# Three edits to one kernel: gated delta net's k normed ahead of q, memory attention's result cut in its last rounds, one sum for two chained norms

## The reference, cut to what matters

```python
qh, kh, vh = l2norm(heads(qc)), l2norm(heads(kc)), heads(vc)     # gated delta net: q and k as unit rows
...
x = x + memory_cross_attention(rmsnorm(x, norm_xa_w), rmsnorm(mem, norm_mem_w), w_xq, w_xkv, w_xo)
#   4 heads of width 256: o = softmax(q k' / 16) v, then o @ w_xo
...
x = x + jnp.square(jax.nn.relu(h @ w_ff1)) @ w_ff2
x = rmsnorm(x, norm_out_w)                # the first block's last step
...
h = rmsnorm_2(x, g_mix); z = h @ w_in_2   # the second block's first
```

## Time and profile before

| what | value |
|---|---|
| runs of the kernel, us | 4253.4, 4267.21, 4269.94 (median 4267.21) |
| profiled execution, its own time | 4255.12 us |
| its span in the profile | 4253.6 us |
| TensorE busy | 3916.8 us (92% of the span) |
| VectorE / ScalarE / GpSimd busy | 2141.3 / 1153.0 / 329.8 us |
| mean granted TensorE clock | 0.943 of full speed |

### The profile page before, as it was taken

How to read it: one execution, slowest core, us unless ns; L and a number is a source line. 1 busy time by engine, 2 the same in 40 slices (tenths; PEclk the granted TensorE clock), 3 DMA queues, 4 the chain that set the end, 5 groups by cost and what they waited for, 6 DMA issues and landing times. The chain is left out here.

```text
span 4253.6 us, 75535 instructions
## 1 busy us (share of the span) xinstructions
PE 3916.8 (92%) x33542; PEld 3211.7 (76%) x33542; DVE 2141.3 (50%) x3526; ACT 1153.0 (27%) x1595; POOL 329.8 (8%) x362
## 2 busy tenths in 40 slices
PE   6999969988989999999999899778887999999999
PEld 5888847777858888888798677666666788888877
DVE  4643335554434444444624332555554476666673
ACT  4221234433323212212400322333323321111132
POOL 0001102330000000000000000231311000000000
PEclk8999979998999999999999899787888999999999
DMA  5211120114121111111232312211005211111111
GB/s 180 89 52 58 55 92 10 29 33 142 45 80 55 50 50 50 50 50 44 98 97 97 122 55 86 82 36 45 23 10 171 89 50 40 60 40 50 50 45 65
DMA packets 212888, 278.83 MB, mean 66 GB/s; under 512 B 15548, under 2 KB 170940, under 8 KB 212436
## 3 DMA queue, kind: packets, MB, share of 16 engines
q1 hardware_dynamic: 181040, 201.84, 14.9%
q10 hardware_dynamic: 31524, 72.16, 4.5%
HBM read 215.54 MB, written 58.43 MB: 64 GB/s over the span
## 5 line engine op out<-in xcount | busy, mean ns | idle before, releaser
L436 PE MATMUL ps<-sb_a_h,sb_whi 128*128 128x512 f32 x2784 | 1105.3, 397 | 6.0 <-DVE sb_wlo L397 5.5
L438 PE MATMUL ps<-sb_a_h,sb_whi 128*128 128x512 f32 x2784 | 1089.6, 391 | 0.0
L437 PE MATMUL ps<-sb_a_h,sb_wlo 128*128 128x512 f32 x2784 | 1089.2, 391 | 0.0
L436 PEld LDWEIGHTS ps<-sb_a_h,sb_whi 128*128 128x128 f32 x2784 | 525.6, 189 | 133.1 <-issue 15.8
L437 PEld LDWEIGHTS ps<-sb_a_h,sb_wlo 128*128 128x128 f32 x2784 | 525.7, 189 | 112.2 <-issue 4.5
L438 PEld LDWEIGHTS ps<-sb_a_h,sb_whi 128*128 128x128 f32 x2784 | 525.0, 189 | 112.5
L389 ACT ACTIVATE sb_whi<-sb_wraw 128x2048 fp32r<-128x2048 f32 (+3 forms) x146 | 260.3, 1783 | 825.1 <-PE ps L438 500.4
L397 DVE TENSOR_TENSOR sb_wlo<-sb_wraw,sb_whi 128x2048 fp32r<-128x2048 f32 (+3 forms) x146 | 313.9, 2150 | 238.9 <-ACT sb_whi L389 218.3
L548 DVE TENSOR_TENSOR sb_x<-sb_x,ps 128x512 f32<-128x512 f32 x480 | 313.5, 683 | 216.5 <-PE ps L438 207.6
L436 PE MATMUL ps<-sb_a_g,sb_whi 128*128 128x512 f32 x896 | 349.7, 390 | 10.5 <-DVE sb_x L548 10.5
L438 PE MATMUL ps<-sb_a_g,sb_whi 128*128 128x512 f32 x896 | 348.6, 389 | 0.0
(11 more groups left out here) (524 smaller groups left out, 5797.9 us busy)
## 6 DMA issues: line engine op xcount, KB each, us to landing
sb_wraw<-w_in SPq DMA_DIRECT2D x33, 1024.0 KB, 5.3
sb_wraw<-w_ff SPq DMA_DIRECT2D x32, 1024.0 KB, 5.3
sb_wraw<-w_up SPq DMA_DIRECT2D x22, 1024.0 KB, 5.1
sb_wraw<-w_down SPq DMA_DIRECT2D x11, 1024.0 KB, 5.0
...
```

Of the source, the lines that this page charges most:

```text
L436: e.matmul(o, wh[:, k, c], xh[:, sl], start=(k == 0), stop=False)
L437: e.matmul(o, wl[:, k, c], xh[:, sl], start=False, stop=False)
L438: m = e.matmul(o, wh[:, k, c], xl[:, sl], start=False, stop=(k == t.nk - 1))
```

## The change

1. Gated delta net. The gate rows are loaded by SyncE at the end of the stage before, ahead of the barrier, and to another place. SyncE loads k, then q, then v. The rows are squared, summed, rooted and multiplied in the order 3, 4, 5, 0, 1, 2: ScalarE does Ln of k's 6 halves, Exp of its 3 rows, then Ln of q's 6 halves and Exp of its 3 rows. The transposes of k wait for the third multiplied row instead of the sixth.
2. Memory attention. Once the last queries are done, SyncE loads the stored rows 0 to 5 back, each onto the place of its own low part. In round 8 rows 0 and 1 are cut, in round 9 rows 2 and 3, in round 10 rows 4 and 5. The results of units 6 and 7 (rows 6 and 7) are no longer stored: ScalarE copies them from the bank to the high part and VectorE subtracts that from the bank. TensorE does two rows of `pe_first` at the end of round 9, two at the end of round 10 (banks 0, 2, 3 and 4) and four after it. The barrier is gone.
3. The two norms. ScalarE makes sqrt(w² + eps) once, in the ninth group of the feed-forward part. The first 8 squares are those of x times it, so that one sum gives the second block's root; `mix_sums` stands after the second tile. The squares of x come after it, and `out_sums` stands after the fifth tile, in the banks of the other.

The diff, cut to what acts (signal declarations and unchanged lines are left out):

```diff
@@ -574,11 +574,11 @@
-def pe_first(e, tiles, x, ready, feats=None, side=None, at=None):
+def pe_first_steps(e, tiles, x, ready, feats=None, side=None, at=None, ring=None):
...
-    ps = [bk.take(t.key, RING) for t in tiles]
+    ps = [bk.take(t.key, ring or RING) for t in tiles]
@@ -594,7 +594,12 @@
+        yield
...
+def pe_first(e, *args):
+    for _ in pe_first_steps(e, *args):
+        pass
 def ac_high_piece(e, q, n, seg, gain):
@@ -612,12 +617,12 @@
-def ac_square_of(e, q, f, seg, sqb):
+def ac_square_of(e, q, f, seg, sqb, gain=1.0):
...
-    e.activation(sqb[(f - 1) % 2] if f else RR, xk(f), ACT.Square).then_inc(*z_sq.up())
+    e.activation(sqb[(f - 1) % 2] if f else RR, xk(f), ACT.Square, scale=gain).then_inc(*z_sq.up())
 def ve_add_square(e, q, f, sqb):
@@ -1295,6 +1300,12 @@
     def sp_a1(e):
...
+        for d in range(2):
+            e.wait_ge(*bk.filled(("ml_d", (d, 7))))
+        for o in gd_g_out:
+            e.wait_ge(*o.at(0))
+        e.dma_start(R(X0 + 7 * T, T, 0, 24), S["gd_g"]).then_inc(*gd_gin.up())
@@ -1479,32 +1491,30 @@
+    UNIT = (3, 4, 5, 0, 1, 2)
...
-    def ac_in(e):
-        e.dma_start(R(X0, T, 0, 24), S["gd_g"]).then_inc(*gd_gin.up())
...
     def sp_in(e):
-        for j in range(3):
+        for j in (1, 0, 2):
...
     def pe_unit_row(e, f):
...
-            e.wait_ge(*un_squared[f % 2].at(f // 2))
+            e.wait_ge(*un_squared[f % 2].at([g for g in UNIT if g % 2 == f % 2].index(f)))
...
     def pe_gates(e):
...
-        e.wait_ge(*gd_gin.at(0))
...
-            m = e.transpose(ps[:, i * 24:(i + 1) * 24], R(X0 + i * 128, 128, 0, 24), C("ident", 0, 24)[:, 0:24])
+            m = e.transpose(ps[:, i * 24:(i + 1) * 24], R(X0 + 7 * T + i * 128, 128, 0, 24), C("ident", 0, 24)[:, 0:24])
@@ -1536,7 +1546,7 @@
-        for f in (1, 3, 5):
+        for f in (3, 5, 1):
@@ -1546,9 +1556,9 @@
-        for f in range(6):
+        for n, f in enumerate(UNIT):
...
-            e.wait_ge(*un_root.at(f))
+            e.wait_ge(*un_root.at(n))
@@ -1576,31 +1586,32 @@
-        for f in (0, 2, 4):
+        for f in (4, 0, 2):
...
-        for f in range(6):
-            for hf in range(2):
-                e.wait_ge(*bk.filled(("gd_un", f, hf)))
-                e.activation(un_rt[f][:, hf * 512:(hf + 1) * 512], bk["gd_un", f, hf], ACT.Ln, bias=EPS,
-                             scale=1.0).then_inc(*bk.empty(("gd_un", f, hf)))
-        for f in range(6):
-            for hf in range(2):
-                e.wait_ge(*bk.emptied(("gd_un", f, hf)))
-            e.activation(un_rt[f], un_rt[f], ACT.Exp, scale=-0.5, bias=LN8 if f < 3 else 0.0).then_inc(*un_root.up())
+        for part in (UNIT[:3], UNIT[3:]):
+            for f in part:
+                for hf in range(2):
+                    e.wait_ge(*bk.filled(("gd_un", f, hf)))
+                    e.activation(un_rt[f][:, hf * 512:(hf + 1) * 512], bk["gd_un", f, hf], ACT.Ln, bias=EPS,
+                                 scale=1.0).then_inc(*bk.empty(("gd_un", f, hf)))
+            for f in part:
+                for hf in range(2):
+                    e.wait_ge(*bk.emptied(("gd_un", f, hf)))
+                e.activation(un_rt[f], un_rt[f], ACT.Exp, scale=-0.5, bias=LN8 if f < 3 else 0.0).then_inc(*un_root.up())
...
-    sp_in(sp), ac_in(ac), pe_gates(pe), ve_gates(ve), ac_gates(ac)
+    sp_in(sp), pe_gates(pe), ve_gates(ve), ac_gates(ac)
...
     def pe_turn(e):
...
-            e.wait_ge(*(un_done.at(5) if f0 == 3 else gd_in[2].at(0)))
+            e.wait_ge(*(un_done.at(2) if f0 == 3 else gd_in[2].at(0)))
@@ -2142,6 +2155,21 @@
+    xos = abreast_last(fm("xo", "w_xo", 0, 1024))
+    first_steps = []
...
+    def raw(k):
+        return R(H0 + (8 + k) * T, T)
...
+    def xo_ready(k):
+        return llo.at(8 + k) if k < 6 else bk.emptied(("xa_o", 7, k - 6))
...
+    HIGHS = [0, 1, (6, 0), (6, 1), 2, 3, (7, 0), (7, 1), 4, 5]
...
+    def xo_high(what):
+        return lhi.at(8 + HIGHS.index(what))
     def pe_xa(e, r):
@@ -2185,6 +2213,12 @@
+        if r == 9:
+            first_steps.append(pe_first_steps(e, xos[:4], hp, xo_ready, None, None, None, (0, 2, 3, 4)))
+            bk.spot[RING] = 5
+        if r >= 9:
+            for _ in range(2):
+                next(first_steps[0])
     def ve_xa(e, r):
@@ -2214,15 +2248,25 @@
-            e.wait_ge(*bk.filled(("xa_o", u, 0)))
-            e.wait_ge(*xo_out[0].at(u - 1))
-            e.tensor_copy(xob[0], bk["xa_o", u, 0]).then_inc(*bk.empty(("xa_o", u, 0)))
+            if u < 6:
+                e.wait_ge(*bk.filled(("xa_o", u, 0)))
+                e.wait_ge(*xo_out[0].at(u - 1))
+                e.tensor_copy(xob[0], bk["xa_o", u, 0]).then_inc(*bk.empty(("xa_o", u, 0)))
+            else:
+                for dv in range(2):
+                    hi, lo = (x[:, span(u % 2)] for x in hp(6 + dv))
+                    e.wait_ge(*xo_high((u, dv)))
+                    e.tensor_tensor(lo, bk["xa_o", u, dv], hi.bitcast(F32), ALU.subtract).then_inc(*bk.empty(("xa_o", u, dv)))
...
+        if r >= 8:
+            for k in (2 * r - 16, 2 * r - 15):
+                e.wait_ge(*xo_high(k))
+                e.tensor_tensor(hp(k)[1], raw(k), hp(k)[0].bitcast(F32), ALU.subtract).then_inc(*llo.up())
     def ac_xa(e, r):
@@ -2249,37 +2293,50 @@
-            e.wait_ge(*bk.filled(("xa_o", u, 1)))
-            e.wait_ge(*xo_out[1].at(u - 1))
-            e.activation(xob[1], bk["xa_o", u, 1], ACT.Copy).then_inc(*bk.empty(("xa_o", u, 1)))
+            if u < 6:
+                e.wait_ge(*bk.filled(("xa_o", u, 1)))
+                e.wait_ge(*xo_out[1].at(u - 1))
+                e.activation(xob[1], bk["xa_o", u, 1], ACT.Copy).then_inc(*bk.empty(("xa_o", u, 1)))
...
+                if u >= 6:
+                    e.wait_ge(*bk.filled(("xa_o", u, dv)))
+                    e.activation(hp(6 + dv)[0][:, span(hf)], bk["xa_o", u, dv], ACT.Copy).then_inc(*lhi.up())
+                    continue
...
+        if r >= 8:
+            e.wait_ge(*lp[r - 8].at(2))
+            for k in (2 * r - 16, 2 * r - 15):
+                e.activation(hp(k)[0], raw(k), ACT.Copy).then_inc(*lhi.up())
...
+    def sp_xo(e):
+        e.wait_ge(*bk.filled(asks[7][-1].key))
+        for k in range(6):
+            for x in xo_out:
+                e.wait_ge(*x.at(k // 2 * 2 + 1))
+            e.dma_start(raw(k), S["xo"][k * 128:(k + 1) * 128, :]).then_inc(*lp[k // 2].up())
...
-    next_phase()
...
-    xos = abreast_last(fm("xo", "w_xo", 0, 1024))
+    sp_xo(sp)
     def ffn_gain(k):
...
     def pe_xo(e):
-        pe_first(e, xos[:4], hp, llo.at)
+        for _ in first_steps[0]:
+            pass
...
     def ve_xo(e):
-        ve_parts(e, 8, hp, bufs)
...
     def ac_xo(e):
-        ac_parts(e, S["xo"], 8, hp, bufs)
@@ -2290,12 +2347,15 @@
-both, gained, gained_sum, out_root = sig("both_gains"), sig("gained_squared"), sig("gained_summed"), sig("out_root")
...
-BOTH = AF2[:, 3584:3592]
-SQ2 = [AF[:, j * T:(j + 1) * T] for j in range(3)]
+both, x_sq, x_sum, out_root = sig("both_gains"), sig("x_squared"), sig("x_squares_summed"), sig("out_root")
+with_eps = sig("gain_with_eps")
+with_eps = sig("gain_with_eps")
...
+BOTH, WITH_EPS = AF2[:, 3840:3848], AF2[:, 3848:3856]
+SQ2 = [AF[:, j * T:(j + 1) * T] for j in range(2)]
 def both_gain(k):
@@ -2366,6 +2426,12 @@
+            if tiles is up[8]:
+                e.activation(WITH_EPS, PB[:, pat["norm_out_w"]:pat["norm_out_w"] + 8], ACT.Square).then_inc(*with_eps.up())
+                e.wait_ge(*with_eps.at(0))
+                e.activation(WITH_EPS, WITH_EPS, ACT.Ln, bias=EPS).then_inc(*with_eps.up())
+                e.wait_ge(*with_eps.at(1))
+                e.activation(WITH_EPS, WITH_EPS, ACT.Exp, scale=0.5).then_inc(*with_eps.up())
@@ -2418,18 +2484,19 @@
-    def sums(e):
-        for hf in range(2):
-            ps = bk.take(("out_rms", hf), RING)
-            e.wait_ge(*z_sa.at(7 * 2 + 6))
-            e.wait_ge(*bk.room(("out_rms", hf)))
-            e.matmul(ps, C("ones"), RR[:, span(hf)], start=True, stop=True).then_inc(*bk.fill(("out_rms", hf)))
+    def mix_sums(e):
...
-            e.wait_ge(*gained_sum.at(6))
+            e.wait_ge(*z_sa.at(7 * 2 + 6))
...
-            e.matmul(ps, C("ones"), SQ2[0][:, span(hf)], start=True, stop=False)
-            e.matmul(ps, EPS.to_broadcast([128, 128]), RR[:, span(hf)], start=False, stop=True).then_inc(*bk.fill(("mix_rms", hf)))
+            e.matmul(ps, C("ones"), RR[:, span(hf)], start=True, stop=True).then_inc(*bk.fill(("mix_rms", hf)))
...
+    def out_sums(e):
+        for hf in range(2):
+            ps = bk.take(("out_rms", hf), (SUM0, SUM1)[hf])
+            e.wait_ge(*x_sum.at(6))
+            e.wait_ge(*bk.room(("out_rms", hf)))
+            e.matmul(ps, C("ones"), XS[:, span(hf)], start=True, stop=True).then_inc(*bk.fill(("out_rms", hf)))
     def root_columns(e):
@@ -2444,8 +2511,10 @@
-            if n == 2:
-                sums(e)
+            if n == 1:
+                mix_sums(e)
+            if n == 4:
```

(14 more changed lines are left out.)

7 lines of the change are left out of this document (4 added, 3 removed).

## The result

| | median us | lowest to highest | runs |
|---|---|---|---|
| kernel before | 4258.77 | 4239.42 to 4269.94 | 16 |
| changed kernel | 4241.43 | 4229.89 to 4256.41 | 16 |

The ratio of the changed kernel's time to that of the kernel before is 0.9966, with a 95% interval of 0.9951 to 0.998: some 14.5 us of 4259 (0.0034 x 4259), the interval from 9 to 21. The two medians stand 17.3 apart, which that interval holds too. It is less than half a per cent, as forecast, and the interval doesn't reach 1. The median lies 12 us under the 4253 forecast and inside the range.

The account below looks back on a forecast made before the run. TensorE, busy 92% of the span, bounds the kernel, so only its waits can give time back; 0.6 + 8.9 + 4.8 = 14.3 us off the three runs' median of 4267.2 gives 4253, range 4232 to 4264.

Parts of the forecast that it names:

- (a): Memory attention and norms: new stalls don't lower the clock or are short; 20.9 us off, 4246; 10%.
- (b): Memory attention's rounds and second block: late cuts, queued products or late weights; about 6.5 us off, 4261; 12%.
- (c): Memory attention: TensorE's clock stays at 1.2 GHz to the end of the eight rows; +11.6 us, 4279; 3%.
- (d): Delta net: two switches at twice 1.28 each make ScalarE later, +2.0 instead of -0.6 us; 4255.6; 5%.
- Part 1: Gated delta net's start: VectorE's last product ends 0.6 us sooner; bounds -2.6 and +2.1.
- Part 2: Memory attention: 12.95 us removed, 4.1 added by new stalls, -8.9; bounds -12.95 and -5.5.
- Part 3: Second block's norm sums: 10.0 us against 14.8, -4.8; bounds -6.5 and 0.
- head start: Delta net's unit rows: TensorE starts their sums 1.2 to 1.3 us sooner, at about 577.1, not 2.6.
- the switches eat the head start: Delta net, ScalarE: two added table loads, 2.56 us, use up the earlier start of the unit rows.
- 12.95: Memory attention, us removed: idle of 10.55 ahead of w_xo and the lower clock behind it, 5.10 against 2.7.

Follow-up runs that it names:

- Experiment 7: Changed kernel with all 12 Ln ahead of all 6 Exp, one table switch instead of three; one run, 4253.27 us, its stretch 44.46 against 44.91.
- experiments 6: Changed kernel with VectorE's square of q's row 1 behind its reads of the gates' sums; one run, 4244.3 us, its stretch 43.28 against 44.91.
- 8: Changed kernel with the delta net's start rebuilt: v turned between k's and q's sums, q multiplied last; 4230.87 us, ratio 0.9934 to the kernel before.

## Why the prediction was right

**The sum.** 14.3 forecast, 14.6 in the three stretches, 14.5 by the runs. Of the cases it was the likeliest: none of (a) to (d) happened. That the three numbers lie so close is partly luck: parts 1 and 2 missed by 0.6 and 0.7 in opposite directions, the interval of the runs reaches from 9 to 21, and the 1.5 us that part 3 gives behind its stretch, which makes 16.1, stand nowhere in the prediction.

**Part 1, -0.6 forecast, 0.0 measured.** The term that was mis-sized is the head start of the unit rows' sums: 1.2 at their first matmul, of which 0.6 and not 1.2 was left at the sixth Ln. The steps came out one by one; the kernel after runs 0.38 later at its issue, which is taken off here. First unit product 577.1 as forecast; sixth Ln ended at 586.0 against 585.4, since the first sums ran at the low clock (24 matmuls 13.32 instead of 12.72) after the longer wait of 4.19; last Exp 599.7 against 599.2; VectorE's sixth product 601.2 against 600.6. The 0.6 that was left of the head start went to that clock. k's transposes did not start ahead of 603, as said: their new wait changed nothing. The reason given, that the switches eat the head start, is half of it. Experiment 7 shows that without them the last Exp ends 1.2 sooner and VectorE's products 0.75, and experiments 6 and 8 that more is to be had from two orders in VectorE's queue: the square of q's row ahead of the gates' sums, and all six products and the small copies ahead of the first read-out.

**Rival (d)** fell with the row: a switch has 1.28 and the next activation starts 1.29 after the load began, in all three places, where double that would have shown as gaps. The Trainium skill, "ScalarE: Activation LUTs", section "What ACT_TABLE_LOAD costs", has 2.66 with a drain of 1.38; this case's traces show the load's part (1.28) and no drain: the load starts within 0.03 us of the end of the activation before it. Its advice to group by set (section "Rules for kernel authors") points the right way but is worth little here: 1.2 us at the last Exp for two switches.

**Part 2, -8.9 forecast, -9.6 measured.** The idle in unit 6 was 3.01 (3.3 forecast), with the clock fallen behind it (1.7 forecast and measured, 3.68 - 1.98), the one in unit 7 1.41 (0.78 + 0.7 forecast). The read-backs stayed hidden, and so did the cuts for w_xo's matmuls: rows 4 and 5 were ready at 1269.6 with the 7.36 taken off, wanted at 1271.0 (1270 and 1271 forecast). The rows 6 and 7, the bank and the clock made the whole difference between 12.95 and what was got. Of the 0.7 that it came out better, 0.3 is the second product of unit 6, which came 2.2 later than before (1258.78 less the 7.36 that this execution is late, against 1249.19) where 2.5 was forecast; the rest lies within the 0.6 by which this stretch varies in kernels without the edit.

**Part 3, -4.8 forecast, -5.0 measured.** Wait 4.39 (4.5), sums 3.61 (3.6), other sums 1.88 (1.9). VectorE's closing norm came at 2092.89; with the 2.21 that the two executions differ by at the four tiles (1289.57 - 1287.36), that is 2095.1 against 2094.6 forecast, and no wait for a block followed. The 1.5 us behind the stretch the prediction didn't have. The sqrt(w² + eps) cost TensorE nothing: ScalarE's five rows in the ninth group fit ahead of the first square, whose idle shrank from 4.19 to 0.96:

```profile
1689.01 0.63 ACT L2445 ACTIVATE sb_a_f<-sb_a_f 128x512 f32<-128x512 f32 x1 [0.96 <-DVE sb_a_f L2415]
```

**What was off** is the level: the three runs of the kernel before had a median 8.4 us above that of the sixteen. The size of the gain was not.
